# K cache pages: heads 4 to 7 turned by VectorE in 32x32 blocks and scored with 32x32 matmuls, heads 0 to 3 by TensorE; tiles of k behind every third pair

## What is computed

```python
k_past = cache_k[page_table]              # 8 sequences x 8 pages x 128 tokens, 8 heads x 128
means  = k_past summed over blocks of 256 tokens / 256
scores = einsum('bqhd,bnhd->bqhn', q, means)      # 3 of 4 past blocks are selected by these
logits = einsum('bqhd,bqhrkd->bqhrk', q, sel_k) * scale - slopes * distance
p      = softmax(concat(logits of the selected blocks, logits of the 8 new tokens))
out    = p @ values of the same pages and tokens
```

## Time and profile before

| | us |
|---|---|
| median of 3 runs | 963.36 (957.81 to 964.37) |
| the profiled execution | 957.88 |
| its span | 956.1 |
| busy in the span: TensorE matmul / VectorE / ScalarE / GpSimd | 915.2 / 629.9 / 438.6 / 72.4 |
| K stage, first transposes to last scores | 445.7 to 572.5 |
| V stage, first values to last | 575.4 to about 671 |

### The profile page before, as it was taken

One profiled execution on the slowest core, in us unless ns is written; L12 is line 12 of the kernel. 1 busy time (PEld: TensorE's weight loads), 2 busy tenths in 40 slices (PEclk: granted clock), 3 DMA queues, 4 the chain that ended last, 5 costly groups with the idle time before them and its releaser, 6 DMA issues.

```text
span 956.1 us, 18901 instructions
## 1 busy us (share of the span) xinstructions
PE 915.2 (96%) x7559; PEld 854.3 (89%) x7559; DVE 629.9 (66%) x1086; ACT 438.6 (46%) x824; POOL 72.4 (8%) x82
## 2 busy tenths in 40 slices
PE   6999998999999999999999999889899999999993
PEld 5999877989999999998888778777899999999992
DVE  5567567868887475677576747434568797657536
ACT  4434663456446254445344453433537635536322
POOL 0000005500000000220000000000120000000042
PEclk9999999999999999999999999999999999999997
DMA  9952313555454453465897998999654445445201
GB/s 284 266 167 94 121 52 77 163 172 173 133 163 147 138 171 134 153 236 202 301 275 262 352 360 307 392 357 393 207 147 153 157 133 167 142 140 168 90 1 55
DMA packets 133931, 181.72 MB, mean 190 GB/s; under 512 B 5811, under 2 KB 116347, under 8 KB 133844
## 3 DMA queue, kind: packets, MB, share of 16 engines
q1 hardware_dynamic: 126810, 175.25, 56.1%
q10 hardware_dynamic: 6394, 3.17, 1.1%
q0 software_dynamic: 640, 2.10, 0.8%
HBM read 174.17 MB, written 6.32 MB: 189 GB/s over the span
## 4 chain that ended last, share of the span: by engine, by line
PE 88%; DVE 4%; DMA 3%; ACT 2%; issue 1%; SPq 1%; ACTq 1%; DVEq 0%
PE ps L518 23%; PE ps L520 23%; PE ps L519 23%; PE ps L787 6%; PE ps L829 3%; DMA page<-in_cache_v_dram 2%; PE ps L881 1%; DMA x_tok<-in_x_sample_dram 1%; PE ps L533 0%; PE ps L677 0%; ACTq L1081 0%; ACT probs_turned L1262 0%; PE ps L866 0%; PE ps L590 0%; DVE gate_o L1423 0%
## 5 line engine op out<-in xcount | busy, mean ns | idle before, releaser
L964 ACT ACTIVATE w_hi<-raw 128x1024 fp32r<-128x1024 f32 x192 | 202.8, 1057 | 250.0 <-PE ps L520 247.9
L1342 DVE TENSOR_TENSOR w_lo<-raw,w_hi 128x1024 fp32r<-128x1024 f32 x192 | 234.9, 1225 | 117.4 <-ACT w_hi L964 117.3
L518 PE MATMUL ps<-x_hi,w_hi 128*128 128x322 f32 (+1 forms) x896 | 282.6, 315 | 0.0
L520 PE MATMUL ps<-x_hi,w_lo 128*128 128x322 f32 (+1 forms) x896 | 279.4, 312 | 0.0
L519 PE MATMUL ps<-x_lo,w_hi 128*128 128x322 f32 (+1 forms) x896 | 278.8, 311 | 0.0
L518 PE MATMUL ps<-h_hi,w_hi 128*128 128x320 f32 x640 | 199.8, 312 | 2.7 <-DVE h_lo L1475 1.7
L520 PE MATMUL ps<-h_hi,w_lo 128*128 128x320 f32 x640 | 198.8, 311 | 0.0
L519 PE MATMUL ps<-h_lo,w_hi 128*128 128x320 f32 x640 | 198.8, 311 | 0.0
L518 PEld LDWEIGHTS ps<-x_hi,w_hi 128*128 128x128 f32 x896 | 170.1, 190 | 5.4 <-ACT k_turned L1228 2.9
L519 PEld LDWEIGHTS ps<-x_lo,w_hi 128*128 128x128 f32 x896 | 170.6, 190 | 0.2
L520 PEld LDWEIGHTS ps<-x_hi,w_lo 128*128 128x128 f32 x896 | 169.4, 189 | 0.0
(11 more groups left out here) (308 smaller groups left out, 925.8 us busy)
## 6 DMA issues: line engine op xcount, KB each, us to landing
raw<-in_w_up_dram SPq DMA_DIRECT2D x32, 1024.0 KB, 5.8
raw<-in_w_down_dram SPq DMA_DIRECT2D x32, 1024.0 KB, 5.3
page<-in_cache_k_dram SPq DMA_DIRECT2D x64, 512.0 KB, 5.4
page<-in_cache_v_dram SPq DMA_DIRECT2D x64, 512.0 KB, 7.1
raw<-in_w_in_a_dram SPq DMA_DIRECT2D x12, 1024.0 KB, 8.8
raw<-in_w_kv_dram SPq DMA_DIRECT2D x8, 1024.0 KB, 6.5
raw<-in_w_out_a_dram SPq DMA_DIRECT2D x4, 1024.0 KB, 5.4
raw<-in_w_q_b_dram SPq DMA_DIRECT2D x4, 1024.0 KB, 5.3
```

Source lines behind the costliest of these rows:

```text
L518: mm(out, WH[t % SPL][:, k, :], hi[:, k, 0:width], start=(k == 0), stop=False)
L520: last = mm(out, WL[t % SPL][:, k, :], hi[:, k, 0:width], start=False, stop=(k == 7))
L964: A(WH[t % SPL][:, :, :], raw[RBUF[u]][:, :, 128 * (t % 2):128 * (t % 2) + 128], ACT.Copy)\
L1342: V.tensor_tensor(WL[t % SPL][:, :, :], raw[RBUF[t // 2]][:, :, 128 * (t % 2):128 * (t % 2) + 128], WH[t % SPL][:, :, :].bitcast(F32), ALU ...
```

## The change

Only heads 0 to 3 of a K page are transposed by TensorE, into one bank, and copied by ScalarE. VectorE turns heads 4 to 7 straight from the page buffer in SBUF, each 32x32 block by itself, into `KD` (128 x 512 a page, four pages to a buffer, two buffers). So partitions 32i to 32i + 31 hold, for tokens 32i to 32i + 31, dimensions of a head in four pieces of 32. `score_quad` scores four pages at once from them: 64 matmuls, for each piece jd, row group i and head j, with a 32x32 weight block of q (`QD`) and 128 columns (32 tokens of four pages); row group i writes bank 4 + i, and the four pieces add up there. `spread_q` copies the pieces of q to all four row groups once, by matmuls with columns of the identity. `score_pair` keeps four matmuls of 256 columns and the other half of bank 4 + r.

Tiles of k stand in pairs 2, 5, ... 23 instead of 2, 4, ... 16, their turns one pair later as before, the new tokens' scores in pair 26 instead of 18. A pair takes two slots, not four. SyncE's units of w_v stand behind pages 24, 36 and 48 instead of 21, 29 and 39. Group 0's exponentials move to pages 59 to 63, two a page; the block maxima and biases move back too. POOL clears four padded tiles instead of two. `logits(G, i)` now reads bank 4 + i with a reduction to eight sums and two products of 256 columns. `q_spread` and `q_block` lay q for the quads on ScalarE. The core of the diff:

```diff
-K_FIRST = 2
-SLOTS = [(p, k) for p in range(NPG // 2) for k in range(5) if k < 4 or K_FIRST <= p <= K_FIRST + 16]
+K_FIRST, K_STEP = 2, 3
+K_TILE = {K_FIRST + K_STEP * n: n for n in range(8)}
+K_TURN = {K_FIRST + K_STEP * n + 1: n for n in range(8)}
+K_OWN = K_FIRST + K_STEP * 8
+SLOTS = []
+for _p in range(NPG // 2):
+    SLOTS += [(_p, 0), (_p, 1)]
+    if _p == 0:
+        SLOTS += [(_p, 2), (_p, 3)]
+    if _p in K_TILE or _p in K_TURN or _p == K_OWN:
+        SLOTS.append((_p, 2))
 SLOT = {pk: i for i, pk in enumerate(SLOTS)}
...
+                    if g < NPG + RING:
+                        sp.wait_ge(s_kB, g - RING + 1)
...
             load_unit(4 * Q_WK + 2)
             load_unit(4 * Q_WK + 3)
-            pages(8, 22)
+            pages(8, 25)
             load_unit(4 * Q_WV)
-            pages(22, 30)
+            pages(25, 37)
             load_unit(4 * Q_WV + 1)
-            pages(30, 40)
+            pages(37, 49)
             load_unit(4 * Q_WV + 2)
-            pages(40, NPG + 9)
+            pages(49, NPG + 9)
             load_unit(4 * Q_WV + 3)
             pages(NPG + 9, NPG + 19)
...
             def turn_page(P):
                 pe.wait_ge(s_in[P % RING], 16 * (P // RING + 1))
+                slot_free(P // 2, P % 2)
+                bank = slot_bank(P // 2, P % 2)
+                for j in range(4):
+                    last = nc.tensor.transpose(bank[:, 128 * j:128 * j + 128],
+                                               page[P % RING][:, 128 * j:128 * j + 128], ident)
+                last.then_inc(s_used, 1)
+            def spread_q():
                 for half in range(2):
-                    k = 2 * (P % 2) + half
-                    slot_free(P // 2, k)
-                    bank = slot_bank(P // 2, k)
-                    for j in range(4):
-                        h = 4 * half + j
-                        last = nc.tensor.transpose(bank[:, 128 * j:128 * j + 128],
-                                                   page[P % RING][:, 128 * h:128 * h + 128], ident)
-                    last.then_inc((s_half, s_used)[half], 1)
+                    slot_free(0, 2 + half)
+                    if half == 0:
+                        pe.wait_ge(s_ev[0], evac(8 * Q_WQ + 7)[1])
+                    for jd in (2 * half, 2 * half + 1):
+                        c = 256 * (jd % 2)
+                        for i in range(4):
+                            last = mm(slot_bank(0, 2 + half)[32 * i:32 * i + 32, c:c + 256]
+                                      .rearrange("p (h t) -> p h t", h=4), ident[:, 32 * jd:32 * jd + 32],
+                                      QA[:, 4:8, TP:T], start=(jd % 2 == 0), stop=True, skip_group_check=True)
...
             def score_pair(pair):
                 G, bb, r = pair // 16, pair // 4 % 4, pair % 4
                 pe.wait_ge(s_kA, 2 * pair + 2)
-                pe.wait_ge(s_kD, 2 * pair + 2)
                 if pair % 16 == 0:
                     pe.wait_ge(s_qz, G + 1)
                 if pair == 0:
                     pe.wait_ge(s_uk, 8)
-                if pair in (16, 18):
-                    pe.wait_ge(s_Lr, 2 + pair - 16)
-                for a_ in range(2):
-                    for j in range(4):
-                        last = mm(ps[SCORE_BANK[2 * a_ + r // 2]][32 * j:32 * j + 32,
-                                                                  256 * (r % 2):256 * (r % 2) + 256],
-                                  QZ[G][:, 4 * a_ + j, bb, :], KT[pair % 2][:, 4 * a_ + j, :],
-                                  start=(bb == 0 and r % 2 == 0), stop=True, skip_group_check=True)
+                if pair in (16, 17):
+                    pe.wait_ge(s_Lr, pair - 16 + 1)
+                for j in range(4):
+                    last = mm(ps[4 + r][32 * j:32 * j + 32, 256:512], QZ[G][:, j, bb, :], KT[pair % 2][:, j, :],
+                              start=(bb == 0 and r < 2), stop=True, skip_group_check=True)
                 last.then_inc(s_sc, 1)
+            def score_quad(c):
+                b, half = divmod(c, 2)
+                G, bb = b // 4, b % 4
+                pe.wait_ge(s_kB, 4 * c + 4)
+                if half == 0:
+                    pe.wait_ge(s_qd, b + 1)
+                if c == 8:
+                    pe.wait_ge(s_Lr, 4)
+                kd = KD[c % 2][:, :, :].rearrange("p g (x t) -> p x g t", t=32)
+                for jd in range(4):
+                    for i in range(4):
+                        for j in range(4):
+                            r = slice(32 * i, 32 * i + 32)
+                            last = mm(ps[4 + i][32 * j:32 * j + 32, 128 * half:128 * half + 128]
+                                      .rearrange("p (g t) -> p g t", g=4),
+                                      QD[j // 2][r, j % 2, jd, bb, :], kd[r, 4 * j + jd],
+                                      start=(bb == 0 and half == 0 and jd == 0 and i >= 2), stop=True,
+                                      skip_group_check=True, tile_position=(32 * i, 32 * j))
+                last.then_inc(s_sd, 1)
...
             for pair in range(NPG // 2):
                 turn_page(2 * pair)
                 turn_page(2 * pair + 1)
+                if pair == 0:
+                    spread_q()
                 if pair >= 1:
                     score_pair(pair - 1)
-                if K_FIRST <= pair <= K_FIRST + 16:
-                    k_extra(pair)
+                if pair >= 2 and pair % 2 == 0:
+                    score_quad(pair // 2 - 1)
+                k_extra(pair)
             score_pair(NPG // 2 - 1)
+            score_quad(NPG // 4 - 1)
             probs_turn(0)
...
+            def q_spread():
+                for half in range(2):
+                    act.wait_ge(s_qr, half + 1)
+                    A(QR[:, 2 * half:2 * half + 2, :, :],
+                      slot_bank(0, 2 + half)[:, :].rearrange("p (j h t) -> p j h t", j=2, h=4), ACT.Copy)\
+                        .then_inc(s_qrc, 1)
...
+            def q_block(b):
+                bb = b % 4
+                act.wait_ge(s_qrc, 2)
+                if b >= 4:
+                    act.wait_ge(s_sd, 2 * bb + 2)
+                for hp in range(2):
+                    ins = A(QD[hp][:, :, :, bb, 8 * bb:8 * bb + 8],
+                            QR[:, :, 2 * hp:2 * hp + 2, 8 * b:8 * b + 8].rearrange("p j h t -> p h j t"), ACT.Copy)
+                ins.then_inc(s_qd, 1)
...
                     ins = A(AO[:, :, 8 * b:8 * b + 8], src, ACT.Copy)
                 ins.then_inc(s_ao, 1)
+            q_lay(0)
             for P in range(NPG):
-                p = P // 2
                 k_copy(P)
-                if P in (1, 3):
-                    q_lay(P // 2)
-                if P % 2 and K_FIRST <= p <= K_FIRST + 16:
-                    k_extra(p)
-                if 45 <= P < 55:
-                    exp_step(0, P - 45)
+                if P == 1:
+                    q_spread()
+                    q_block(0)
+                if P in (3, 4, 5):
+                    q_block(P - 2)
+                if P == 6:
+                    q_lay(1)
+                if P in (14, 22, 30, 38):
+                    q_block(4 + (P - 14) // 8)
+                if P % 2:
+                    k_extra(P // 2)
+                if P >= 59:
+                    exp_step(0, 2 * (P - 59))
+                    exp_step(0, 2 * (P - 59) + 1)
...
-            def k_copy(P):
-                dve.wait_ge(s_used, P + 1)
-                if P >= 4:
-                    dve.wait_ge(s_sc, P // 2 - 1)
-                V.tensor_copy(KT[P // 2 % 2][:, 4:8, 128 * (P % 2):128 * (P % 2) + 128],
-                              slot_bank(P // 2, 2 * (P % 2) + 1)[:, :].rearrange("p (h t) -> p h t", h=4))\
-                    .then_inc(s_kD, 1)
+            def k_blocks(P):
+                dve.wait_ge(s_in[P % RING], 16 * (P // RING + 1))
+                if P >= 8:
+                    dve.wait_ge(s_sd, P // 4 - 1)
+                V.transpose(KD[P // 4 % 2][:, P % 4, :], page[P % RING][:, 512:1024]).then_inc(s_kB, 1)
...
-            def logits(G, c):
-                bsum = parts(G)[0]
-                bank = ps[SCORE_BANK[c]]
-                V.tensor_reduce(bsum[:, 2 * c:2 * c + 2], bank[:, :].rearrange("p (n k) -> p n k", n=2),
-                                AX.X, ALU.add)
-                V.scalar_tensor_tensor(L[G][:, c // 2, 512 * (c % 2):512 * (c % 2) + 512],
-                                       keys[:, 512 * (c % 2):512 * (c % 2) + 512], slope[:, c // 2:c // 2 + 1],
-                                       bank[:, :], ALU.mult, ALU.add).then_inc(s_Lr, 1)
+            def logits(G, i):
+                bank = ps[4 + i]
+                V.tensor_reduce(qsum[:, 8 * i:8 * i + 8], bank[:, :].rearrange("p (n k) -> p n k", n=8), AX.X, ALU.add)
+                V.scalar_tensor_tensor(L[G][:, 1, :].rearrange("p (g x t) -> p g x t", g=8, x=4)[:, :, i, :],
```

(23 more changed lines are left out.)

## The result

| | before | after |
|---|---|---|
| median of 4 runs, us | 960.59 (957.32 to 964.37) | 978.87 (972.44 to 980.99) |
| profiled execution / its span, us | 957.88 / 956.1 | 980.49 / 978.7 |
| first transposes of a page to first values, us | 445.7 to 575.4: 129.8 | 444.4 to 591.3: 147.0 |
| first to last values of a page, us | 95.0 | 100.8 |

The ratio is 1.018 (95% interval 1.011 to 1.025): slower, where 944 us were forecast. Of the 22.6 us between the two spans 17.2 lie in the K stage, 5.8 in the V stage, 1.0 behind it; 1.3 are won ahead of it.

The account below looks back on a forecast made before the run. TensorE was taken to bound the kernel. Removed 46.4 less quads 19.2 and spreading q 1.9 left 25.3 us; less 8.2 of waits, 17, so 957.9 becomes 941, median 944 us; own case 936 to 950, range 932 to 962.

Parts of the forecast that it names:

- Removed work: Taken off TensorE per quad in the K stage: 16 transposes (1.90 us) and half the scores (1.00), together 2.90 us.
- The quad's price: A quad's 64 matmuls, sixteen tiles at once, take 1.0 us on TensorE, plus 0.2 allowed for changing tile form.
- Rival 1: Only eight tiles work together in a quad, so it takes 2.0 + 0.2 us; 953 us in all; chance 0.20.
- (a): VectorE, with block transposes at 0.69 us each, comes late in pairs 5 to 12 with rebuilding; 2 us.
- (d): ScalarE's ten exponentials, moved to pages 59 to 63, delay copies; the last pair's scores wait about 3.3 us.
- (b): Turns of k tiles, one pair behind their tile, wait where no quad lies between: four times some 0.4, 1.6 us.
- (c): Group 0's logits wait for quad 7: 0.6 us, and 0.7 more at pair 18; 1.3 us.
- (e): K pages are covered on average; nothing counted, though the last six pairs ask 520 GB/s.
- rival 4: Pages come late at the K stage's tail and the V stage's start; 951 us; chance 0.12.
- (f): The V stage keeps its work near its DMA limit; it should shift, not shrink, still some 97 us long.
- rival 2: Issue or weight loading sets a quad's pace at 29 ns an instruction, 3.75 us a quad; 977 us; chance 0.12.
- turning point: In rival 2, from 20 ns per instruction upwards a quad costs the 2.8 it and its share of spreading remove.

Follow-up runs that it names:

- e2_piece1: Changed kernel with one of the four 32-dimension pieces in each quad, 64 TensorE instructions instead of 256; 941.72 us, ratio 0.983 to the kernel before.
- e5_small_pages: Changed kernel loading 128 instead of 1024 columns of each K page from page 8 on, TensorE's instructions all the same; 960.44 us (one run).
- e8_shift96: Changed kernel with 48 more transposes (96 TensorE instructions, results unused) ahead of the first page's transposes; 988.2 us (one run).
- e10_rows_inner: Changed kernel with a quad's two inner loops exchanged, so neighbouring matmuls lie in different row groups; 976.37 us (one run).
- e9_octs_spread: Changed kernel with waits eased, eight pages scored by 64 matmuls of 256 columns, logits spread, rebuilding of x moved; 955.77 us, ratio 0.9955 to the kernel before.
- e3_wide: Changed kernel with every second quad left out and the others on 256 columns (the same 128 twice); 956.74 us, ratio 0.996 to the kernel before.
- e1_cols64: Changed kernel with each quad matmul on 64 columns instead of 128, same number of instructions; 978.84 us, ratio 1.022 to the kernel before.

## Why the prediction was wrong

**What bounds the kernel: right.** TensorE sets the end of the K stage before and after, and e2_piece1 shows that time off its list comes out of the total: with a quad at 0.45 the kernel took 941.7 us.

**Removed work: a little too high.** 2.90 us per quad were to go. The pair's scores cost 0.57, not 0.50, and a pair's transposes 1.02 where no tile lies ahead of them, not 0.95. (Behind a tile or its turns the transposes take 0.87.) Over the stage, added up from one matmul's start to the next in e5_small_pages, whose clock stayed at 1.00, it makes 2.9 us for the scores and 1.7 for the transposes beyond half of what they took before.

**The quad's price: the step that failed first.** "I take 1.0, because each group of rows fits tiles times columns and none shows an issue limit, and allow 0.2." It is 1.83: 16 x 0.63 = 10 us. Rival 1 has the right size (2.0 + 0.2) and the wrong reason; columns are worked on 16 tiles at once, and a fixed 7 ns for every matmul instruction, with its weight load, comes on top. That fixed part was in reach: own scores at 14 ns each were set aside as bound by their tiles, though no row told the two apart. The Trainium skill ("TensorE: Matmul & The Clock Gate", section "Wait — 56ns, not 53.3ns?") gives a floor of about 25 ns from start to start, however small the matmul; by it a quad would have been 3.2 us. It does not hold here for neighbours on different tiles: 1.64 us from first to last start of a quad is 13 ns each, and 0.25 us for the 32 of e2_piece1 is 8.

**The term that was missing: 13.5 us.** TensorE's instructions come in blocks of 256 by a DMA queue of their own. In the K stage before, 10 such blocks were brought in 126 us; after, 21 in 141 us (packets, MB, share of the DMA engines). The row of before, then that of after:

```profile
q8 instruction: 10, 0.16, 0.5%
```

```profile
q8 instruction: 21, 0.34, 0.9%
```

Before, a block lasted 9.8 to 14.4 us and always outlasted the transfer of the next. A quad's 128 matmul instructions and their 128 weight loads are one whole block; in e5_small_pages, where little holds them up, the blocks of the stage last 2.5 to 8.8 us. Beside pages at 280 GB/s on average the transfer is late nine times. That this is the cause is shown by three runs: without most of the traffic (e5_small_pages) 4.0 us are left, with the ends moved (e8_shift96) the pieces move, with a quarter of the added instructions (e2_piece1) there are none. The forecast counted 128 instructions a quad, without the weight loads, priced only their run time, and never asked how they reach the engine.

**The clock.** In the K stage the granted clock was 1.00 before and 0.95 after, that is four stretches at the 1.2 GHz level, 3.4 us each (from 458.9, 547.7, 568.2 and 581.8 us), behind pieces of idleness. At half rate they cost up to 4 x 1.7 = 6.8 us. The traces bear it out: from one matmul's start to the next, with all waits taken out, TensorE's list of the stage takes 125.7 us in the changed kernel and 118.3 in e5_small_pages, which has the same instructions and a clock of 1.00 throughout, 7.4 less. But it doesn't follow from the idle time alone: e10_rows_inner had 14.9 us of "issue" in the stage and one such stretch. So it belongs to the loss, with a size that changes from run to run, and which piece brings it is open.

**The waits.** (a) and (d) are about the right size for the wrong reasons. (a) had 2 us behind the rebuilding of x in pairs 5 to 12; the one wait for a block transpose, 1.1 us before 543.1, stands behind the block maxima of group 0 in VectorE's queue, a reduction of 2.27 us. (d) had 3.3 us behind the exponentials at the end; the waits for k copies, 3.1 us, are six over the stage, four of them behind stores of a turned tile in ScalarE's queue, and the last alone, 0.28 us, behind exponentials. (b) four turns of 0.4: three of 0.48. (c) logits about 1: none in the profiled execution, which fits a TensorE that comes later. (e) No page is waited for in the K stage. But as soon as TensorE is quick, in e2_piece1 and e9_octs_spread, 1.7 us of page waits are there: rival 4 begins to be true where the gain would be.

**The sum again.** Forecast for the K stage: 129.8 - 17 = 112.8. Measured 147.0, so 34.2 more: issue 13.5, quads 10.8, clock 7.4, scores 2.9, transposes 1.7, and 2.0 less of other waits (7.7 us, where 8.2 were added to the 1.5 of before). These are the sums over the records named above, so the quads' 10.8 stands beside the 10 of the chain. In e5_small_pages the stage is 130.5 us, 16.5 less: 9.6 of issue and 7.4 of clock, against 0.5 more of other waits. So the supply of instructions is the largest term and the quad's price the next.

**(f) The V stage: 5.8 us longer in the profiled execution.** It should have shifted unchanged. The largest new wait is 5.8 us for `p_logit` (1.2 before), and behind it stands ScalarE:

```profile
645.34 7.58 ACTq L1132
...
654.47 0.27 DVE p_logit L1737
...
654.79 0.48 PE ps L771
```

One of three stores of v that ScalarE issues (line 1132) held its queue for 7.58 us, where the same one held it for 2.77 before; the exponentials of the prompt's attention are queued behind it. In the other runs it held 3.4 to 5.3 us, and 8.6 in e3_wide, whose V stage took 101.8 us; with 3.4 in e1_cols64 it took 94.3, less than before. So the loss comes and goes with one store, and that the change brings it is not shown. Then the granted clock fell for 10.2 us (0.74 over 650 to 670 in the windows above). Why the issue takes so long, whether for want of room beside the pages' transfers, was not tried.

**Chances.** Slower had 0.14 and was given to an issue limit (rival 2, 977 us). That 977 and 979 lie so close is luck. Rival 2 had 41 us more from quads of 3.75, less 8 of waits; the quads brought about 10, and the rest is the supply of blocks and the clock, which no rival had. Its mechanism holds in part: a fixed price for each instruction is there, but 7 ns beside the columns, 14 in all and not 29. (Its turning point, 2.8 us a quad, is 22 ns an instruction, not 20.)

## What to carry to other kernels

Count the instructions of a change beside its columns: small tiles divide the columns' time by the tiles that work together, but every matmul keeps a fixed price (7 ns here), so widen each of them (256 columns for eight pages instead of 128 for four) before splitting finer. Then look how long 256 instructions of the engine last against the load on the DMA engines; beside the pages nine blocks with 2.2 to 5.7 us of work ran dry, though not every one of that length, and the blocks of 9.8 us and more never did. "issue" in the middle of a run of like matmuls, with no wait, is the sign of it, and moving the code by some instructions shows whether it is.

## What the runs showed of the hardware

- A VectorE transpose of 128x512 f32 in 32x32 blocks from SBUF to SBUF takes 683 ns, as much as a copy of so many columns.
- f32 matmuls on sixteen 32x32 tiles overlap fully in their columns (5.8 to 5.9 ns a column for 128 matmul instructions together, from 64 to 256 columns), with 7 ns more for each matmul instruction and its weight load.
- TensorE's instructions come in 16 KB for 256, semaphore waits and weight loads counted. The transfer takes 0.9 to 1.4 us, starts 0.5 to 5.2 us into the running block when pages are loading, and TensorE, where it has run dry, goes on 1.2 to 1.6 us after its end. With 108 instead of 280 GB/s of traffic the pieces shrink from 13.5 to 4.0 us, of which 2.9 lie where whole pages load again.
- The issue of a store by ScalarE's queue took from 0.6 to 8.6 us beside page traffic, the third of three like stores always the longest (2.8 us or more).
